# Pairs of gate tiles in the second mixer: six pairs in place of twelve plain tiles, and later taps in the second MLP

## What is computed

```python
z = h @ w_in[l]                                   # h = rmsnorm(x, ln_mix_g)
qa, ka, va, qb, kb, vb, rb, gk_lr, ga, gb = split_cols(z)
...
merged = jax.nn.sigmoid(ga) * (ya @ w_branch_a[l]) + jax.nn.sigmoid(gb) * (yb @ w_branch_b[l])
x = x + merged @ w_out[l]
h = rmsnorm(x, ln_ffn_g[l])
a, u = jnp.split(h @ w_ffn_in[l], 2, axis=-1)
a = causal_dwconv(a, conv_w[l], conv_b[l])
x = x + (jax.nn.silu(a) * u) @ w_ffn_out[l]
```

## Time and profile before

| | |
|---|---|
| median of three executions | 1427.76 us |
| profiled execution, its own time | 1427.68 us |
| its span | 1425.9 us |
| TensorE busy | 1413.9 us (99%) |
| VectorE, ScalarE, POOL busy | 986.4, 647.0, 214.8 us |
| granted TensorE clock, mean | 0.998 |
| loads | 130 MB, mean 91 GB/s |

### The profile page before, as it was taken

How to read it: one execution, slowest core, us unless ns; L and a number is a source line. 1 busy time by engine, 2 the same in 40 slices (tenths; PEclk the granted TensorE clock), 3 DMA queues, 4 the chain that set the end, 5 groups by cost and what they waited for, 6 DMA issues and landing times.

```text
span 1425.9 us, 20562 instructions
## 1 busy us (share of the span) xinstructions
PE 1413.9 (99%) x8054; PEld 1213.9 (85%) x8054; DVE 986.4 (69%) x1537; ACT 647.0 (45%) x1028; POOL 214.8 (15%) x136
## 2 busy tenths in 40 slices
PE   9999999999999999999999999999999999999998
PEld 6776798889989888887799888888888889999997
DVE  5777477876676657897696736534452888888877
ACT  5345535534345434545464546323332545455450
POOL 4175224000000011330052104000021000000000
PEclk9999999999999999999999999999999999999999
DMA  6222212333233332222211211323323233333331
GB/s 242 89 75 69 65 60 89 100 97 115 93 100 104 119 104 74 89 67 82 74 60 41 65 45 59 110 90 101 98 90 92 87 105 103 103 93 116 104 106 73
DMA packets 36352, 130.00 MB, mean 91 GB/s; under 512 B 4040, under 2 KB 4296, under 8 KB 36256
## 3 DMA queue, kind: packets, MB, share of 16 engines
q1 hardware_dynamic: 35968, 128.44, 28.5%
q10 hardware_dynamic: 288, 0.26, 0.1%
HBM read 126.56 MB, written 2.10 MB: 90 GB/s over the span
## 4 chain that ended last, share of the span: by engine, by line
PE 91%; DVE 5%; ACT 2%; issue 1%; DMA 1%; ACTq 0%; DVEq 0%; SPq 0%
PE P L1728 17%; PE P L1730 16%; PE P L1729 16%; PE P L1709 5%; PE P L1711 5%; PE P L1710 5%; PE P L1776 4%; PE P L1767 4%; PE P L1769 4%; PE P L2069 2%; DVE WL L2561 1%; PE P L1816 1%; PE P L1817 1%; PE P L1818 1%; PE P L1924 1%
## 5 line engine op out<-in xcount | busy, mean ns | idle before, releaser
L2156 ACT ACTIVATE WH<-WR 128x1024 fp32r<-128x1024 f32 x212 | 223.6, 1055 | 259.2 <-PE P L1730 181.4
L2561 DVE TENSOR_TENSOR WL<-WR,WH 128x1024 fp32r<-128x1024 f32 x196 | 265.5, 1355 | 103.0 <-ACT WH L2156 102.6
L1728 PE MATMUL P<-AH,WH 128*128 128x512 f32 x456 | 186.2, 408 | 0.2 <-DVE BC L3002 0.2
L1730 PE MATMUL P<-AH,WL 128*128 128x512 f32 x456 | 178.2, 391 | 0.0
L1729 PE MATMUL P<-AL,WH 128*128 128x512 f32 x456 | 177.8, 390 | 0.0
L1728 PE MATMUL P<-FH,WH 128*128 128x512 f32 x432 | 168.5, 390 | 0.5 <-issue 0.3
L1729 PE MATMUL P<-FL,WH 128*128 128x512 f32 x432 | 168.4, 390 | 0.0
L1730 PE MATMUL P<-FH,WL 128*128 128x512 f32 x432 | 168.1, 389 | 0.0
L3375 POOL TENSOR_TENSOR AC<-AC,SQ 128x512 f32<-128x512 f32 x27 | 42.5, 1573 | 506.7 <-ACT SQ L2211 505.8
L1709 PE MATMUL P<-AH,WH 128*128 128x256 f32 x400 | 113.5, 284 | 0.3 <-ACT SN L2167 0.2
L1711 PE MATMUL P<-AH,WL 128*128 128x256 f32 x400 | 113.2, 283 | 0.0
(11 more groups left out here) (409 smaller groups left out, 3148.0 us busy)
## 6 DMA issues: line engine op xcount, KB each, us to landing
WR<-in_ws SPq DMA_DIRECT2D x212, 512.0 KB, 3.5
WX<-in_ws SPq DMA_DIRECT2D x21, 512.0 KB, 3.5
out<-Y SPq DMA_DIRECT2D x8, 256.0 KB, 2.0
H<-in_xT SPq DMA_DIRECT2D x3, 512.0 KB, 8.0
C<-in_const SPq DMA_DIRECT2D x1, 946.5 KB, 11.0
H<-in_xT SPq DMA_DIRECT2D x2, 256.0 KB, 4.4
PR<-in_pT SPq DMA_DIRECT2D x1, 512.0 KB, 4.9
WR<-in_ws SPq DMA_DIRECT2D x1, 384.0 KB, 4.8
```

The costliest lines, as they stand in the source:

```text
L1728: e.matmul(P, wh, xh, start=start, stop=False)
L1730: ins = e.matmul(P, wl, xh, start=False, stop=stop)
L2156: e.activation(H, w_source(m, order, k), ACT.Copy).then_inc(*at.up("w_hi", "w_hi", k))
L2561: e.tensor_tensor(L, w_source(m, order, k), H, ALU.subtract).then_inc(*at.up("w_lo", "w_lo", k))
```

## The change

Twelve of the sixteen gate tiles (gate_b 0 to 7, gate_a 4 to 7) are computed as six pairs; gate_a 0 to 3 stay plain. The branch_a tiles 4 to 7 now come before their gates: ScalarE copies them out of PSUM (branch_a_copy) and VectorE multiplies them in SBUF later (gated_a). The forms for stage "4" are made beside branch_a 4 to 7 (raws, then splits), behind the end of the normalisation, in buffers of their own. The chunk of branch_a's last blocks is padded (align), and the pad at the same place of the second MLP falls away, so that the plan has 1872 blocks in both kernels. In the second MLP's plain tiles 4 to 7 the steps conv(f) come four blocks behind ffn_a instead of two. Some semaphores are shared between the two attentions.

```diff
         for m in range(8):
...
-            self.finish((lambda: self.yb == 8) if m < 4 else (lambda: self.gated))
-            self.say("branch_a", m, t)
+            if m < 4:
+                self.finish(lambda: self.yb == 8)
+            if m == 4:
+                self.finish()
+                self.beside(self.raws("4", 1))
+            self.say("branch_a" if m < 4 else "branch_a_copy", m, t)
             self.close(t)
-            if m < 6:
-                gate_a(m + 2)
...
+            if m < 2:
+                self.last_plain["4"] = gate_a(m + 2)
+            if m == 5:
+                self.beside(self.splits("4", range(1, 5), 2))
         self.finish()
-        for m in range(8):
+        self.banks = (0, 1, 2, 3, 6, 7)
+        self.align()
+
+        def post(p):
+            kind, i = p.f
+            self.say("gate_first", p, kind, i)
+            self.say("gate_sig", kind, i)
+            yield 1
+            self.say("gate_second", p, kind, i + 1)
+            self.close(p.x)
+            self.say("gate_sig", kind, i + 1)
+            yield 2
+            if kind == "a":
+                self.say("gated_a", i)
+                yield 1
+                self.say("gated_a", i + 1)
...
+        def merged(m):
+            yield 10 if m < 7 else 1
+            self.say("merged_split", m)
+        pair("b", 0)
+        branch(0)
+        pair("a", 4)
+        branch(1)
+        pair("b", 2)
+        branch(2)
+        pair("a", 6)
+        branch(3)
+        for m in (4, 6):
+            pair("b", m)
+            branch(m)
+            branch(m + 1)
+        self.finish()
...
-            self.paced(lambda: None, lambda: None, lambda: conv(f))
+            self.paced(lambda: None, lambda: None, lambda: None, lambda: None, lambda: conv(f))
...
-            w.wait_ge(*at("rbc", "25"[b - NRAW]))
+            w.wait_ge(*at(*(("rbc", "2"), ("rbc", "5"), ("yb", 7))[b - NRAW]))
...
     def t_u(s):
         w.wait_ge(*at("rbc", s))
+        if s == "4":
+            w.wait_ge(*at("ya", 3))
...
         w.wait_ge(*at(("t_diff", "t_2", "t_3", "t_4")[j - 1], s))
+        if s == "4" and j < 4:
+            w.wait_ge(*at("x_lo", "Z2", 2 * j - 1))
...
+    def branch_a_copy(i, t):
+        w.wait_ge(*at("full", t.id))
+        w.wait_ge(*at("yb", 7))
+        if i >= 4:
+            w.wait_ge(*at("gn_gated", 7))
+        e.activation(m.MG[:, i, :], m.bank[t.bank][:], ACT.Copy).then_inc(
...
     def t_2(s):
+        if s == "4":
+            w.wait_ge(*at("yb", 7))
```

More of the change, by code:

```diff
@@ L224, in __init__ @@
         extra = {}
-        for s, buffer in (("2", NRAW), ("5", NRAW + 1)):
+        for s, buffer in (("2", NRAW), ("5", NRAW + 1), ("4", NRAW + 2)):
             mine = [c for c, at in sections if at == s]
@@ L393, in forms, with raws, splits @@
     def forms(self, s, n=5):
+        yield from self.raws(s, 3)
+        yield from self.splits(s, range(1, n), 3)
+    def raws(self, s, pace):
         self.say("t_diff", s)
-        yield 4
+        yield pace + 1
         self.say("t_u", s)
-        yield 3
+        yield pace
         self.say("t_2", s)
-        yield 3
+        yield pace
         self.say("t_3", s)
-        yield 3
+        yield pace
         self.say("t_4", s)
-        yield 3
-        for j in range(1, n):
+        yield pace
+    def splits(self, s, js, pace):
+        for j in js:
             self.say("t_split", s, j)
-            yield 3
+            yield pace
     def narrow(self, name, c0, n, kind):
@@ L1096, in mixer2 @@
             self.close(t)
-            if m < 6:
-                gate(m + 2)
+            self.beside(merged(m))
+        def merged(m):
[14 more added lines that the diff above has]
+        self.finish()
+        self.banks = (0, 1, 2, 3)
         for m in range(8):
@@ L1530, in sn, with gate @@
     def sn(self, s):
-        return self.SN1 if s == "2" else self.SN2
+        return {"2": self.SN1, "4": self.SN3, "5": self.SN2}[s]
+    def gate(self, kind, i):
+        return self.GA[:, i % 2, :] if kind == "a" else self.GB[:, i % 4, :]
     def snap(self, p, j, n=1):
@@ L2482, in gate_a, with gate_sig, merged_split @@
         e.activation(g, g, ACT.Sigmoid).then_inc(*at.up("gate_sig", "ga_sig", i))
-    def gate_b(i, t):
-        g = m.GB[:, i % 4, :]
-        w.wait_ge(*at("gate_b", i))
-        e.activation(g, g, ACT.Sigmoid).then_inc(*at.up("gate_sig", "gb_sig", i))
-    def branch_b(i, t):
+    def gate_sig(kind, i):
+        g = m.gate(kind, i)
+        w.wait_ge(*at("gate_" + kind, i))
+        e.activation(g, g, ACT.Sigmoid).then_inc(*at.up("gate_sig", "g%s_sig" % kind, i))
+    def branch_a_copy(i, t):
[4 more added lines that the diff above has]
+        e.activation(m.MG[:, i, :], m.bank[t.bank][:], ACT.Copy).then_inc(
+            *at.up("branch_a_copy", "branch_a_copy", i))
+        at.also(("branch_a_copy", i), "read", t.id)
+    def merged_split(i):
         w.wait_ge(*at("merged", i))
@@ L2536, in scalar_program @@
            "st_ref": st_ref, "st_scale0": st_scale0, "st_turn": st_turn, "gla_out": gla_out, "gn_square": gn_square,
[L2537 to L2538 removed]
+           "gn_out": gn_out, "vb": vb, "rb_silu": rb_silu, "ya_split": ya_split, "gate_a": gate_a, "gate_sig": gate_sig, "branch_a_copy": branch_a_copy,
+           "merged_split": merged_split, "ffn_a": ffn_a, "ffn_u": ffn_u}
     for name, *a in order.steps:
@@ L3329, in vector_program @@
            "st_mm": st_mm, "gn_rsqrt": gn_rsqrt, "gn_out": gn_out, "gn_lo": gn_lo, "rb": rb, "ya_split": ya_split,
-           "gate_a": gate_a, "branch_a": branch_a, "gate_b": gate_b, "branch_b": branch_b, "mix2": mix2, "ffn_a": ffn_a,
+           "gate_a": gate_a, "branch_a": branch_a, "gated_a": gated_a, "gate_first": gate_first, "gate_second": gate_second, "branch_b": branch_b, "merged_split": merged_split, "mix2": mix2, "ffn_a": ffn_a,
            "ffn_u": ffn_u, "down2": down2, "y_base": y_base}
```

104 lines of the change are left out of this document (71 added, 33 removed).

## The result

The changed kernel takes 1432.39 us (median of 7 runs, 1431.01 to 1432.92), the kernel before 1427.30 (7 runs, 1426.52 to 1428.62): a ratio of 1.0032, 95% interval 1.0021 to 1.0043. So it is 5 us slower, 0.3%, and the interval keeps clear of 1; the forecast was 1.1 us more. The profiled execution took 1432.92 us, with a span of 1431.1 against 1425.9.

A forecast was written before the change was run, and what follows sets the result against it. The prediction took TensorE, busy 1413.9 of 1425.9 us, to bound the kernel. Its terms, -4.9 + 6.5 - 0.5 = +1.1 us on 1427.68, gave 1428.8 us, range 1425.6 to 1431.5.

The forecast's parts named there:

- Step (1): Second mixer: twelve gate tiles become six pairs, taking 4.9 us off TensorE's own time.
- step (2): Forms made beside branch tiles 4 to 7: three waits in the second mixer's first pair, 6.5 us more, bounds 0 and 8.8.
- Wait 1: TensorE idle 3.9 us ahead of the second mixer's first product, until VectorE's remainder of its weights is done.
- The last product's 0.8: Last product of the second mixer's first pair waits 0.8 us for a ScalarE copy queued behind WH<-WS.
- 1.8 us of wait at product 6: Third product of the second mixer's first pair waits 1.7 us, 1.8 with the slow first matmul.
- the clock falls: Rival, chance 0.11: the idle ahead of the second mixer's first product drops TensorE to 1.2 GHz, 2.6 us more, 1431.4.
- Steps (3) and (4): The five later mixer pairs, and the change's copies, POOL work, loads, shared semaphores and last splits: all costed at 0.
- Step (5): Second MLP: wait ahead of the third F2 tile goes, later taps move nothing; -0.5 us, between -0.9 and 0.
- Every pair waits: Rival, chance 0.09: VectorE nearly full, so each of five later mixer pairs pays 0.45 us; 2.3 more, 1431.1.
- The forms are hidden: Rival, chance 0.11: ScalarE reaches t_u by 908 us, so next to nothing of the 6.5 us is left; 1422.3.

The follow-up runs named there:

- e5: Changed kernel with sixteen 512-column matmuls, their result unused, filling TensorE's wait between the last branch tile and the second mixer's first pair: ratio 1.0030.
- e2: Kernel before with only the taps of the second MLP's plain tiles moved to four blocks behind instead of two: ratio 0.9988.
- e1: Changed kernel with the taps of the second MLP's plain tiles put back to two blocks behind: ratio 1.0034.
- e6: Changed kernel with two empty blocks ahead of the second MLP, restoring the chunk cut short there (1880 blocks in all): ratio 1.0010.
- e8: Changed kernel with forms begun one branch tile earlier, splits in order 1, 2, 4, 3, and two empty blocks ahead of the second MLP: ratio 0.9993.
- e10: e8 with the second form's low part on GpSimd, the fourth split ahead of the third, and the third behind the remainder WL<-WX: ratio 0.9995.
- e11: e8 with VectorE's splits in order 1, 4, 2, then the remainder WL<-WX, then 3, without GpSimd: 1425.01 us, ratio 0.9984.
- e7: Changed kernel with forms begun one branch tile earlier and the fourth split ahead of the third: ratio 1.0007.
- e3: Kernel before with the weight stream filled up to a whole chunk ahead of the second MLP, nothing else moved: ratio 1.0011.
- e4: Changed kernel with the second mixer's forms begun one branch tile earlier: ratio 1.0005.

## Why the prediction was wrong

**Step (1), the pairs.** 4.9 us less, and it was: the five later pairs took 10.07 each, and what the first took beyond that is step (2)'s. Only the 0.03 us by which the tile behind each pair grows was left out, 0.18 in all. (The 7.0 us that the prediction names beside it for six pairs should be 7.2, six times its 1.2; it took no part in the sum.)

**Step (2), the forms.** Forecast 6.5 more, measured 6.62. Wait 1: 3.9 forecast, 3.93 measured, released by the row named. The last product's 0.8 was 0.88 with the slow first matmul. In between the make-up was another: not 1.8 us of wait at product 6 but some 1.5 us of slow matmuls and then 0.3 of wait. The prediction named the limit of product 6 rightly, but had the clock at full speed. The sum came out right because both run into the same moment: product 6 could not start before form 4's remainder, whether TensorE got there slowly or stood there. e5 shows it.

**The rival "the clock falls"** happened and cost nothing. I priced it at 2.6 us by adding slow matmuls to a chain that was already waiting, and by holding the clock low past product 6; the matmuls were back at 0.12 us from 927.42 on, ahead of product 6, and a slow matmul took 0.21 us, not the 0.24 of the estimate. The Trainium skill's page "TensorE: Matmul & The Clock Gate", section "HAM oscillation — how this bites in real kernels", says that an idle stretch between bursts re-throttles the array. The trace agrees (0.50 granted after 3.77 us idle), and adds that the penalty counts only where TensorE is what others wait for. The prediction also read the clock as 1.00 from the stretches of the earlier trace rows alone: at 199 us the kernel before falls to 0.50 itself, behind single-column matmuls.

**Steps (3) and (4).** All at 0: the row-by-row difference of the two timelines stays at 3.15 to 3.18 us from the end of the last gate pair to the second MLP's first F2 tile.

**Step (5) failed.** It said -0.5 for the second MLP, bounds -0.9 and 0, and "the taps being two blocks later by themselves move nothing on VectorE's order: 0". Measured: the wait ahead of the third F2 tile went, -0.6; but the pairs waited 2.7 us more, so the step came to +2.1 where -0.5 was forecast. That is 2.6 of the 4.0 us by which the forecast missed the medians' difference; 0.3 are steps (1) and (2), and the 1.1 left is not explained. The 2.7 by the runs, in three terms:

- the later taps, -1.2 (1.23 to 0.00, e2). They do move something: the remainder of the chunk starts 1.2 us earlier in the pair. (With the chunks as the change has them they gain nothing, 3.31 without and 3.94 with, e1.)
- the loads, 0.2 us longer in every build of the change, +1.1 (0.00 in e2 to 1.13 in e6, the same order of steps). One profile each, and its cause is open. e8, e10 and e11, with e6's blocks, have 1.75, 1.32 and 1.50, so this term is 1.1 to 1.8.
- the cut chunk lost, +2.8 (1.13 in e6 to 3.94), or 2.2 if e8 is set against e7 (1.75 to 3.96).

The terms are not independent, and their sizes hang on the order in which they are taken. With the taps last, the borders come to +1.2 (1.23 to 2.44, e3), the build with its slower loads to +0.9 (3.31, e1) and the taps to +0.6 (3.94). Either way the lost cut is the largest.

I had seen the chunks' borders move and counted only what that took from one wait. The sentence "Late next is the first pair's chain of weight sums ... and could take it all back: 0" named the right chain, and then bounded it by the gain that it followed. A chain that is 0.33 us late already has no slack, so each microsecond of delay in it is a microsecond: the remainder starting 0.84 us later (2.65 for 1.81) and the load's chain being 0.38 longer (4.53 for 4.15) make the first pair's 1.22 more. The bound was VectorE's lag there, 5 us by the prediction's own reading, and not zero.

**Rivals.** "Every pair waits" did not happen in the mixer. "The forms are hidden" is what e11 comes close to.

## What to carry to other kernels

When an edit shifts where a stream of weight chunks is cut, list every later place where a cut, or its absence, sets how early the next load starts, and follow remainder, load, sum, copy, product there in time. If that chain has a wait already, its bound on the slow side is not zero. Before pricing slow matmuls or a wait, ask which event they run into: two costs that end at the same release are one cost.

## What the runs showed of the hardware

- The clock's fall is not a matter of the length of a wait alone. After 3.77 us of idle it fell (the change). After 2.38 (e4), 1.87 (e7) and 1.91 (e10) it did not. In e8, whose program differs from e7's here only in numbers of lines, it fell after 1.86:

```profile
922.16 0.28 PE L1775 MATMUL P<-TH,WL 128*128 128x256 f32 x1
924.30 0.58 PE L1773 MATMUL P<-TH,WH 128*128 128x256 f32 x1 [1.86 <-ACT SN L2231]
924.67 0.41 PE L1774 MATMUL P<-TL3B,WH 128*128 128x256 f32 x1
```

  It cost nothing in e8 either: the first pair costs 3.64 us there and 3.66 in e7, where product 6 waits for the same copy and the last product then waits 1.28 us, a wait that e8 does not have.
- The clock can fall with hardly any idle time: in each of the thirteen profiles it fell to 0.50 for some 3 us behind at least one of the two groups of sixteen single-column matmuls (from 190 us, or from 199 to 200), and no idle stretch of TensorE that a row names ahead of it there is above 0.3 us. No run varied these matmuls.
- GpSimd's tensor_tensor holds up VectorE's for nearly its whole length (e10: 3.81 us for 1.67, so 2.14 more, beside one of 2.53). The Trainium skill's page "SBUF — State Buffer", section "🔬 SBUF: two separate sides", says this of the port pair that the two share: an exclusive lock, where the other blocks in full. The trace agrees.
- A whole build can have loads that are 0.2 us slower than another's (3.6 to 3.7 against 3.4 to 3.5 for 512 KB), in stretches whose instructions are the same. In a chain without slack that went with 1.1 us. The cause is not known.
